# The order of evacuations and weight pieces on ScalarE and VectorE in a four-layer fp32 stack

## The reference

```python
# first block, per layer
h = rmsnorm(x, norm_mix_pre); q, k, v, g_ret, sc_b, sc_c, sc_x, cf_a, cf_b, gates = split(h @ w_in)
y_ret = (silu(g_ret) * groupnorm(retention(rotary(q), rotary(k), v))) @ w_ret_out
y_sc  = (sc_b * causal_dwconv(sc_c * sc_x)) @ w_sc_out            # 3 taps
y_cf  = silu(layernorm(causal_dwconv(cf_a * sigmoid(cf_b)))) @ w_cf_out   # 31 taps
x = x + rmsnorm((sigmoid(gates) weighted sum of the three) @ w_o)
up = causal_dwconv(rmsnorm(x) @ w_up); gate, val = split(up)      # 3 taps, 2 x 2816 channels
x = x + rmsnorm((silu(gate) * val) @ w_down)
# second block, per layer
xn = rms(x)
m_qk = silu(causal_conv(xn @ w_m_qk) + b); y_a = sigmoid(m_o) * rms(mlstm(m_q, m_k, m_v, gates))   # 4 taps
y_b = attention over the 64 best keys by an index score; y_c = difference of two softmax attentions
x = x + (sigmoid(gates) weighted sum of y_a, y_b, y_c through w_branch) @ w_out
x = x + (silu(g) * u) @ w_down,  g, u = split(rms(x) @ w_gate_up)
```

## Time and profile before

| what | value |
|---|---|
| median of 3 runs | 1883.28 us (1882.15 to 1890.07) |
| profiled execution | 1890.45 us, of which the span is 1888.7 us |
| mean granted clock of TensorE | 0.987 |
| busy: TensorE, VectorE, ScalarE, GpSimd | 96%, 72%, 57%, 10% |
| HBM, mean over the span | 165 GB/s |

### The profile page before, as it was taken

One profiled execution on the slowest core, in us unless ns is written; L12 is line 12 of the kernel. 1 busy time (PEld: TensorE's weight loads), 2 busy tenths in 40 slices (PEclk: granted clock), 3 DMA queues, 4 the chain that ended last, 5 costly groups with the idle time before them and its releaser, 6 DMA issues.

```text
span 1888.7 us, 36583 instructions
## 1 busy us (share of the span) xinstructions
PE 1821.0 (96%) x14784; PEld 1777.7 (94%) x14784; DVE 1361.3 (72%) x2385; ACT 1077.2 (57%) x1812; POOL 186.1 (10%) x200
## 2 busy tenths in 40 slices
PE   8999999999999999999999999999998998999998
PEld 8999999999999999999889889999988998899998
DVE  6997788867898778866757767655567677666553
ACT  5456656655455666654676675554456767645442
POOL 1012310001003410001111003000002100020000
PEclk9999999999999999999999999999998999999999
DMA  7545535554545435553435534455543473345552
GB/s 278 181 149 190 170 143 189 192 201 153 177 157 183 166 144 190 190 202 134 155 134 186 185 114 154 170 197 184 201 153 138 140 206 135 123 146 197 185 188 102
DMA packets 90344, 320.10 MB, mean 169 GB/s; under 512 B 10528, under 2 KB 12992, under 8 KB 90048
## 3 DMA queue, kind: packets, MB, share of 16 engines
q1 hardware_dynamic: 90176, 317.75, 48.8%
HBM read 310.60 MB, written 1.08 MB: 165 GB/s over the span
## 4 chain that ended last, share of the span: by engine, by line
PE 68%; DVE 17%; ACT 9%; issue 4%; POOL 1%; DMA 1%; SPq 0%; DVEq 0%; ACTq 0%; POOLq 0%
PE big L579 61%; PE small L579 5%; DVE L L1094 5%; ACT H L1868 4%; DVE POOL L1356 2%; DVE POOL L1352 2%; PE small L578 2%; DVE POOL L1321 1%; DVE POOL L1451 1%; DVE POOL L1370 1%; ACT POOL L2046 1%; DMA POOL<-POOL 1%; POOL POOL L2464 1%; ACT POOL L2251 0%; DVE POOL L1650 0%
## 5 line engine op out<-in xcount | busy, mean ns | idle before, releaser
L579 PE MATMUL big<-HH,H 128*128 128x256 f32 x3344 | 954.1, 285 | 8.7 <-DVE gates L1338 5.7
L579 PE MATMUL big<-HL,H 128*128 128x256 f32 x3344 | 937.6, 280 | 3.7 <-DVE HL L1229 3.6
L579 PE MATMUL big<-HH,L 128*128 128x256 f32 x3344 | 936.4, 280 | 0.0
L1868 ACT ACTIVATE H<-F 128x1024 fp32r<-128x1024 f32 x582 | 611.1, 1055 | 408.4 <-PE big L579 403.7
L1094 DVE TENSOR_TENSOR L<-F,H 128x1024 fp32r<-128x1024 f32 x574 | 700.8, 1229 | 184.8 <-ACT H L1868 183.7
L579 PEld LDWEIGHTS big<-HH,H 128*128 128x128 f32 x3344 | 635.5, 190 | 13.8 <-DVE gates L1338 6.4
L579 PEld LDWEIGHTS big<-HL,H 128*128 128x128 f32 x3344 | 637.2, 191 | 7.9 <-DVE HL L1229 5.5
L579 PEld LDWEIGHTS big<-HH,L 128*128 128x128 f32 x3344 | 634.3, 190 | 0.0
L579 PE MATMUL big<-FH,H 128*128 128x256 f32 x848 | 241.7, 285 | 4.7 <-ACT POOL L2034 4.7
L579 PE MATMUL big<-FH,L 128*128 128x256 f32 x848 | 237.7, 280 | 0.0
L579 PE MATMUL big<-FL,H 128*128 128x256 f32 x848 | 237.6, 280 | 0.0
(11 more groups left out here) (239 smaller groups left out, 1809.1 us busy)
## 6 DMA issues: line engine op xcount, KB each, us to landing
F<-in_stream SPq DMA_DIRECT2D x582, 512.0 KB, 3.5
POOL<-POOL SPq DMA_DIRECT2D x32, 128.0 KB, 3.9
POOL<-head_rows SPq DMA_DIRECT2D x8, 256.0 KB, 4.9
X<-in_x SPq DMA_DIRECT2D x2, 512.0 KB, 4.1
POOL<-POOL SPq DMA_DIRECT2D x16, 64.0 KB, 2.4
out_x<-X SPq DMA_DIRECT2D x1, 1024.0 KB, 3.9
POOL<-in_decay SPq DMA_DIRECT2D x1, 768.0 KB, 11.1
POOL<-POOL SPq DMA_DIRECT2D x8, 96.0 KB, 5.1
```

The lines of the kernel that those rows point to most:

```text
L579: return pe.e.matmul(out_, lhsT, rhs, start=start, stop=stop)
L1868: a.activation(H[:, j % NR, :], F[:, j % NF, :], ACT.Copy).then_inc(s_hi, 1)
```

## The change

On ScalarE, settle(n - 1) always stands ahead of the high parts of `first`, except where the norm has already made it. On VectorE, settle(n - 1) stands ahead of the low parts where group n - 1 is a gate or value group of the FFN in the first block's two layers (`tapped`); elsewhere its order stays. No instruction is added or removed.

```diff
--- before.py
+++ after.py
@@ -1829,9 +1829,12 @@
                 first, rest = pieces_in(g)
                 if not made_after and full_banks(n - 1):
                     settle(n - 1, begun_pieces(n) + AHEAD - 3)
+                tapped = g.layer < 2 and n > 0 and G[n - 1].members[0].label in ("fg", "fv")
+                if not made_after and tapped and not full_banks(n - 1):
+                    settle(n - 1)
                 for j in first:
                     low_parts(j + AHEAD)
-                if not made_after and not full_banks(n - 1):
+                if not made_after and not tapped and not full_banks(n - 1):
                     settle(n - 1)
                 for j in rest:
                     if not full_banks(n):
@@ -2384,12 +2387,10 @@
                 for name in needed(g):
                     beside.finish(name)
                 first, rest = pieces_in(g)
-                if not made_after and full_banks(n - 1):
+                if not made_after:
                     settle(n - 1)
                 for j in first:
                     high_parts(j + 1 + AHEAD)
-                if not made_after and not full_banks(n - 1):
-                    settle(n - 1)
                 for j in rest:
                     if not full_banks(n):
                         high_parts(j + 1 + AHEAD)
```

## The result

The changed kernel takes 1877.53 us (median of 17 runs, 1864.11 to 1890.42), the kernel before 1884.85 in the same comparison (17 runs, 1876.58 to 1900.73). The ratio is 0.9949, 95% interval 0.9926 to 0.9971: 9.6 us less, between 5.5 and 13.9. The profiled execution has a span of 1873.3 us at a mean granted clock of 0.989. ScalarE's lines after the diff count 3 more: L1871 is the high part, L2037 and L2049 the FFN's evacuations, L1993 that of the convolutions, L2161 was L2158. SyncE's count 1 more: L2583 is the load of F, L2608 the swap. In the experiments, too, a line's number moves by a few with the edit (L1360 in the last one is L1356).

The account below looks back on a forecast made before the run. TensorE's matmuls, in flight 1821.0 of 1888.7 us, were taken as the bound. Terms 4.7 + 1.24 + 2.7 + 1.3 + 1.24 = 11.2 us, taken from the 1883.28 median, gave 1872.1 us, range 1862 to 1884.

Parts of the forecast that it names:

- The loop in the FFN: First block's FFN: ScalarE and VectorE wait in a circle, 5.50 us per pair against TensorE's 5.42; the edit ends the backlog.
- Both waits go: -4.7: First down group in each first-block layer: TensorE's two waits for the gate evacuation vanish, 4.7 us less, bounds 0 and 4.7.
- the clock's 1.24: Behind the second layer's wait at down: the half-clock stretch goes with the wait, 1.24 us less, bounds 0 and 1.24.
- rival 4: One FFN stage changes its matmul pace, 6.7 us either way on top of the forecast: 1865 or 1879; chance 0.1.
- -2.7 for two: Convolutions of q and k, second block's layers: small gaps behind high parts go, 1.36 us per layer, 2.7 for two.
- The 0.75: Convolutions of q and k: VectorE's taps wait 0.75 us for an evacuation behind a high part; evacuating first removes it.
- -1.3: Retention, first block's second layer: earlier copies bring the swaps forward, TensorE's longest L1411 wait falls 1.3 us, bounds 0.66 and 1.7.
- another -1.24: Retention, first block's second layer: the half-clock stretch behind the L1411 wait goes too, 1.24 us less, bounds 0 and 1.24.
- the second swap's 0.66: Retention, first block's second layer: VectorE's 0.66 us wait at the second swap, claimed to go once its copy comes earlier.
- no other SP work is passed: Retention, first block's second layer: the earlier swap overtakes nothing in SP's queue, as the F load before it was already issued.
- Rival 1: Evacuation was already hidden and waits move to what was second to last: 1883 us; chance 0.15.
- Rival 2: Only the FFN pays, 4.7 to 5.9 us; other links hold the convolution and retention chains: 1877 to 1879; chance 0.25.

Follow-up runs that it names:

- the timed halves: ScalarE's reorder only in the first block's FFN, and only outside it, each against the kernel before: ratios 1.0004 and 0.9989.

## Why the prediction was right, and where a step failed

Forecast 1872.1, range 1862 to 1884; measured 1877.5. The direction held and the value lies in the range; of the steps, not all did. That the sum of 11.2 us lies within the measured 5.5 to 13.9 is in part luck, as one term was twice too large, one did not come in the changed kernel's profile, and one was too small.

- **The loop in the FFN**: shown. With the evacuation first the period is TensorE's 5.44 in place of 5.50, and no wait remains in any of the four quick stages that had ScalarE's half. What the forecast did not see is that ScalarE's half alone does it, while VectorE's half leaves the loop at 5.51 and shows no gain in time.
- **"Both waits go: -4.7"** was mis-sized. The forecast took the two waits of one profile as the kernel's. They were a draw: both FFN stages had the quick pace there, in the next profile of the same kernel neither. At nine quick stages in 18 the expected value is about half, 2.3 (an estimate), and with it some half of the clock's 1.24. The trace had a warning, the two paces of the earlier trace rows, and the forecast carried that over to the time of whole stages only (rival 4), not to whether the loop falls behind at all.
- **Convolutions, "-2.7 for two"**: 25.41 to 23.80 is 1.6 per layer, 3.2 for two, in every kernel with ScalarE's half there, and 25.4 in those without. The 0.75 went, as forecast; a wait of 1.85 later in the same chain, which the forecast did not count, fell to the 0.91 shown above. TensorE's waits for L2161 and L1572 lost only 1.8 in sum against the 2.7 looked for, and nothing with ScalarE's half outside the FFN; that a TensorE that comes earlier waits longer would account for it, but is not shown. The half-clock stretches there the forecast left in place, for waits above 1.5. They did stay: 17 to 24 us of half clock in five profiles with the old order, 14 to 21 in five with the new; but no run shows such a bound, and in the earlier trace rows one of two waits of 2.3 has no half clock behind it.
- **Retention, "-1.3" and "another -1.24"**: failed in the profile of the changed kernel, L1411's longest wait being 2.3. The step was that the second swap's 0.66 "goes as well, since its copy too stood behind a high part", on top of "no other SP work is passed". The second swap stood behind a load of F, and that load behind a low part, which VectorE makes only after the first swap; ScalarE's early copy of k could not bring it forward. The copy of q did bring the first swap forward, yet its landing varied between 4.0 and 6.0 us from execution to execution; why was not found. In two profiles with ScalarE's half (alone, and outside the FFN) it landed in some 4.2 and the second layer's wait was 0.8 and 0.7, as forecast; in the changed kernel it took 5.8. But in those two the first layer's swap was the late one (5.6 and 6.0), and its wait for L1411, of which the forecast counted nothing, rose from 1.0 to 1.8 and 2.2. Over both layers the waits sum to 3.1 to 5.4 us in five profiles without ScalarE's half here and 2.6 to 2.9 in four with it (the early swaps left out), so about 1 us is seen of the 1.3 (an estimate from so few profiles); the half-clock stretch behind the second layer's wait is there in all five and in one of the four. With the swaps moved ahead of the load the forecast's wait came out in both layers.
- **Rival 1**, evacuation hidden already, is out: the rule of the Trainium skill ("Perfetto Trace Analysis", section "Matmuls"), by which groups rotated through banks let evacuation overlap the next group's matmuls, held inside the stage at either pace, and at the slow pace at the down group also; it failed at the quick pace where two banks are taken at once. Without the weave it held again, in one quick stage.
- **Rival 2** came nearest beside the forecast: 2.3 + 0.6 + 3.2 for FFN, clock and convolutions, and about 1 for retention with up to 0.9 for its clock, give 6 to 8 us, against the 7.3 between the medians and the 9.6 of the ratio. This sum is worked out from traces; the timed halves are too near to 1 to confirm it.

## What to carry to other kernels

Before a wait is priced from one profile, find out whether the profile's pace made it: two loops that differ by 1.5% (5.42 and 5.50 here) trade places when the pace changes by 4%, so the wait's price needs its frequency as well as its length. The circle between two engines was cut here by moving one piece, the high part, out of it; the reorder on the other engine only put one low part in the place of another. And when a transfer is to start earlier, read the queue ahead of it: what releases the instruction in front of it may be the very engine that waits for the transfer.

## What the runs showed of the hardware

At a granted clock of 1.00, TensorE runs the same stream of fp32r matmuls at one of two paces, 0.1133 or 0.1178 us each. The pace holds through a whole stage of 100 us and more, and changes at interruptions, shown by the stalls that were put in. An FFN with its down product is 1584 matmuls, so 1584 x 0.0045 = 7.1 us for each of four layers. Four such draws could make up to 28 us, about the 26 over which 35 runs of the kernel before scatter (1874.38 to 1900.38); that they do is not shown. Its two profiles do not bear it out by themselves: the one with both first-block FFNs quick has the longer span (1888.7 and 1887.0), as it has the two waits as well. What picks the pace at a restart was not found: in the windows above, neither DMA share nor granted clock sets those of one pace apart from those of the other.
